# The last projection of a mixer walks its weight blocks outermost and its token tiles innermost

## The chip, the cores and the metric

The kernel runs on 1 core of a Trainium2 chip. The metric is the device time of one execution in microseconds; the median of 3 runs is given. A smaller time is better.

## What is computed

One layer of a decoder for 256 tokens with 1024 channels: a mixer (a gated convolution branch and a differential attention branch, whose gated sum goes through a last projection `w_o`), and then a feed-forward part with 32 experts, of which each token takes 4. What matters for this case is the seam between the two:

```
mix = (sigmoid(g_conv) * y_conv + sigmoid(g_attn) * y_attn) @ W_o
x   = x + gate1 * mix
h2  = RMSNorm(x) * (1 + scale2) + shift2
x   = x + gate2 * MoE(h2)     # top-4 of 32 experts, clamped SwiGLU,
                              # softmax over the selected router logits
```

Everything is in 32-bit floats.

## The kernel before

The 256 tokens are two tiles of 128 (`TT = 2`, index `tt`). Weights pass through one large area of SBUF, cut into 11 slots of 2 MB each. In the mixer, weight blocks of 1024 x 512 go round in six of these slots; `w_o` is the last two blocks, `WO0` and `WO0 + 1`, each with one half of the 1024 output columns. After the mixer the slots take the experts' weights: an expert has six chunks of 2 MB, four of `w_up` and two of `w_down`, so 192 chunks come in through the queue of SyncE, in a fixed order, each when its slot is free.

The order of the work is written by hand. Each engine has its own program, and semaphores join them. The list `order` numbers the uses of four PSUM banks; use n takes bank n % 4, `bank_full` tells that TensorE has filled it and `bank_free` that it was read. The four `w_o` results are uses `WO_USE` to `WO_USE + 3`.

What happens around the last projection, engine by engine:

- TensorE transposes the mixed tokens (line 1241), then makes the four results of `w_o` (line 1253, 8 matmuls of 128x512 each, which the trace records as 16): tile 0 with block 0, tile 0 with block 1, tile 1 with block 0, tile 1 with block 1. Then for each token tile: it copies x into the output accumulators by two matmuls with the identity (line 1261), waits for h2 of this tile, transposes h2 (line 1269, 8 transposes), waits for ScalarE's copies, and makes the router logits (line 1276, recorded as 16 matmuls of 32 columns). After both tiles come the routing steps (lines 1283 to 1313), and then the loop over units of at most 32 tokens of an expert (lines 1321 to 1386).
- VectorE multiplies each `w_o` result by the gate (line 939) and adds it to x (line 941). In the same pass over the tiles it finishes the norm: reciprocal (944), scale (945), shift (947). So the h2 steps of tile 0 stand ahead of the `w_o` results of tile 1. After both tiles it makes the second gate (951) and the routing from the logits (956 on).
- ScalarE squares and sums x of a tile (655), takes the square root (657), copies the transposed h2 of this tile (661), and goes to the next tile only then.
- SyncE's queue issues the experts' chunks. After chunks 0 to 5 it waits until block `WO0` was used and loads chunk 6, waits until `WO0 + 1` was used and loads chunk 7, waits for the second gate (`gate2_ready`) and loads chunk 8, waits for the last transpose of h2 and loads chunk 9, and waits for the routing's result (`units_ready`) and loads chunk 10. From chunk 11 on, each load waits until TensorE has used the chunk that lay in its slot, in the loop over the units.

The result of the gate multiply lies in `conv_acc`, of which the version before uses two parts in turn.

Of the kernel before, what the change touches and what calls it, by code (L numbers as in the profile page):

```python
# [24 lines left out]
ALU = mybir.AluOpType  # L25
# [5 lines left out]
TT = T // P  # L31
# [39 lines left out]
def build(nc, x, c, positions, w_ada, b_ada, norm1_g, w_in, conv_w, conv_b, conv_ln_g, conv_ln_b,  # L71
# [3 lines left out]
    with ctx:  # L75
# [3 lines left out]
        def sem(name):  # L79
            return ctx.enter_context(nc.semaphore(name))  # L80
# [5 lines left out]
        def slot(i, a=0, b=BLOCKF):  # L86
            return W[:, BLOCKF * i + a:BLOCKF * i + b]
# [11 lines left out]
        conv_acc = slot(X_SLOT, 0, 2 * D).rearrange("p (k t) -> p k t", k=KD)  # L99
        x_tok = slot(X_SLOT, 2 * D).rearrange("p (t d) -> p t d", t=TT)  # L100
# [3 lines left out]
        def small(shape, dt=F32):  # L104
# [131 lines left out]
            sem(n) for n in ("on_ready", "lam_arg"))  # L236
        conv_done, csq_ready, ln_ready, sw_sig, swish_ready = (
            sem(n) for n in ("conv_done", "csq_ready", "ln_ready", "sw_sig", "swish_ready"))
        gate_ready, mixed, x1_ready, h2_ready = (
            sem(n) for n in ("gate_ready", "mixed", "x1_ready", "h2_ready"))  # L240
        lg_ready, tw_ready, routed_ready, comb_ready, m_ready, oh_ready, units_ready = (
            sem(n) for n in ("lg_ready", "tw_ready", "routed_ready", "comb_ready", "m_ready",
                             "oh_ready", "units_ready"))
# [34 lines left out]
        WO0 = len(blocks)  # L278
# [3 lines left out]
        def place(n):  # L282
            return (n + SHIFT) % RING

        def blk(n, k=KD):
            return W[:, place(n) * BLOCKF:(place(n) + 1) * BLOCKF].rearrange("p (k n) -> p k n", k=k)
# [4 lines left out]
        def used_by(n, use):  # L291
            used[n] = (bank_full[use % 4], use // 4 + 1)
# [44 lines left out]
        WO_USE = use_of["w_o", 0]  # L337
# [9 lines left out]
        def gate_use(h):  # L347
            return use_of["gate", h]
# [16 lines left out]
        for i in range(2):  # L365
            used_by(ADA0[i] + 3, ADA_USE[i])
            used_by(V0 + i, V_USE + 2 * i + 1)
            used_by(COUT0 + i, YC_USE[2 * i + 1])
            used_by(AOUT0 + i, YA_USE + 2 * i + 1)
            used_by(WO0 + i, WO_USE + 2 + i)  # L370

        def bank(use):
            return PS[use % 4]

        def full(eng, use):
            eng.wait_ge(bank_full[use % 4], use // 4 + 1)

        def fill(pe, use):
            if use >= 4:
                pe.wait_ge(bank_free[use % 4], use // 4)  # L380
# [139 lines left out]
        def _(act_e):  # L520
# [86 lines left out]
            for h in range(HEADS):  # L607
                par = h % 2
                act_e.wait_ge(s_max, h + 1)
                for part in range(2):  # L610
                    sc = PS[4 + 2 * par + part]
                    for blk_q, (a, b) in enumerate(((0, P), (P, 3 * P))):
                        at = 2 * blk_q + part
# [4 lines left out]
                use = gate_use(h)  # L618
# [32 lines left out]
            load(norm2_b, norm2_g.to_broadcast([P, D]), in_norm2)  # L651

            for tt in range(TT):
                act_e.wait_ge(x1_ready, 2 * tt + 2)
                s.activation(buf_c[:, tt, :], x_tok[:, tt, :], ACT.Square, accum_out=ssq[:, tt:tt + 1]).then_inc(x_ssq, 1)
                act_e.wait_ge(x_ssq, TT + 2 + 2 * tt)
                s.activation(rstd[:, tt:tt + 1], ssq[:, tt:tt + 1], ACT.Sqrt, scale=1.0 / D, bias=eps[:]).then_inc(x_ssq, 1)
                for i in (2 * tt, 2 * tt + 1):
                    use = H2T_USE[i]
                    full(act_e, use)  # L660
                    s.copy(h2T[:, 4 * (i % 2):4 * (i % 2) + 4, P * tt:P * tt + P],
                           bank(use)[:, :].rearrange("p (k t) -> p k t", k=4)).then_inc(bank_free[use % 4], 1)
# [28 lines left out]
        def _(dve):  # L691
            v = nc.vector
            n = 0

            def step(ins):
                nonlocal n
                n += 1
                ins.then_inc(dve_step, 1)
                dve.wait_ge(dve_step, n)
# [43 lines left out]
            for k, (turn, add) in enumerate(((0.25, TWO_PI / 4), (0.0, 0.0))):  # L743
                r, t = rope[:, 4 + k, :, :], rope[:, 1, :, :]
# [76 lines left out]
            for i in range(8):  # L821
                use = QK_USE + i
                tt, col, which = i % 2, NB * ((i // 2) % 2), i // 4
# [39 lines left out]
            for h in range(HEADS):  # L863
                par = h % 2
                dve.wait_ge(sc_full, h + 1)
                for blk_q, (a, b) in enumerate(((0, P), (P, 3 * P))):
                    for part in range(2):
                        at = 2 * blk_q + part
# [52 lines left out]
            for i in range(4):  # L921
                use = YA_USE + i
# [7 lines left out]
            dve.wait_ge(mod_ready, 16 * 16)  # L930
            dve.wait_ge(in_norm2, 16)
            step(v.scalar_tensor_tensor(modb[:, 2, :], modb[:, 2, :], 1.0, norm2_b, ALU.add, ALU.mult))
            for tt in range(TT):
                for half in range(2):
                    cs = slice(NB * half, NB * half + NB)
                    use = WO_USE + 2 * tt + half
                    full(dve, use)
                    gated = conv_acc[:, 2 * half:2 * half + 2, :].rearrange("p a t -> p (a t)")
                    v.tensor_tensor(gated, bank(use)[:, :], modb[:, 0, cs], ALU.mult).then_inc(bank_free[use % 4], 1)
                    dve.wait_ge(bank_free[use % 4], use // 4 + 1)  # L940
                    v.tensor_tensor(x_tok[:, tt, cs], x_tok[:, tt, cs], gated, ALU.add).then_inc(x1_ready, 1)

                dve.wait_ge(x_ssq, TT + 3 + 2 * tt)
                step(v.reciprocal(rstd[:, tt:tt + 1], rstd[:, tt:tt + 1]))
                step(v.scalar_tensor_tensor(h2[:, tt, :], x_tok[:, tt, :], rstd[:, tt:tt + 1], modb[:, 2, :],
                                            ALU.mult, ALU.mult))
                v.tensor_tensor(h2[:, tt, :], h2[:, tt, :], modb[:, 1, :], ALU.add).then_inc(h2_ready, 1)
# [5 lines left out]
            for tt in range(TT):  # L953
                use = LG_USE[tt]
# [108 lines left out]
        def _(pe):  # L1063
            t = nc.tensor

            def wait_block(n):
                pe.wait_ge(blk_full[place(n)], 16 * loads_before[n])
# [33 lines left out]
            for k in range(KD):  # L1101
                use, n0 = CONV_USE + k, CONV0 + 2 * (k // 4)
# [35 lines left out]
            for i in range(8):  # L1138
                use = QKT_USE + i
# [34 lines left out]
            for h in range(HEADS):  # L1174
# [13 lines left out]
                n = GATE0 + h // 2  # L1188
# [32 lines left out]
            for i in range(4):  # L1221
                use = OT_USE + i
# [12 lines left out]
            for i in range(4):  # L1235
                use = MT_USE + i
# [3 lines left out]
                    kk = 4 * (i % 2) + k  # L1240
                    ins = t.transpose(bank(use)[:, P * k:P * k + P], gates[:, i // 2, P * kk:P * kk + P], ident[:])
                ins.then_inc(bank_full[use % 4], 1)
            wait_block(WO0)
            wait_block(WO0 + 1)
            for i in range(4):
                use = WO_USE + i
                fill(pe, use)
                tt, n = i // 2, WO0 + i % 2
                if n == WO0:
                    for j in (2 * tt, 2 * tt + 1):  # L1250
                        pe.wait_ge(bank_free[(MT_USE + j) % 4], (MT_USE + j) // 4 + 1)
                for k in range(KD):
                    ins = t.matmul(bank(use)[:, :], mixT[:, k, P * tt:P * tt + P], blk(n)[:, k, :],  # L1253
                                   start=(k == 0), stop=(k == KD - 1))
                ins.then_inc(bank_full[use % 4], 1)
            pe.wait_ge(in_moe, 16)
            for tt in range(TT):

                pe.wait_ge(x1_ready, 2 * tt + 2)
                for i in range(2):  # L1260
                    t.matmul(Y[tt][i][:, :], ident[:], x_tok[:, tt, NB * i:NB * i + NB], start=True, stop=True,
                             skip_group_check=True)
                pe.wait_ge(h2_ready, tt + 1)
                for i in (2 * tt, 2 * tt + 1):
                    use = H2T_USE[i]
                    fill(pe, use)
                    for k in range(4):
                        kk = 4 * (i % 2) + k
                        ins = t.transpose(bank(use)[:, P * k:P * k + P], h2[:, tt, P * kk:P * kk + P], ident[:])
                    ins.then_inc(bank_full[use % 4], 1)  # L1270
                for i in (2 * tt, 2 * tt + 1):
                    pe.wait_ge(bank_free[H2T_USE[i] % 4], H2T_USE[i] // 4 + 1)
                use = LG_USE[tt]
                fill(pe, use)
                for k in range(KD):
                    ins = t.matmul(bank(use)[:, 0:EXPERTS], h2T[:, k, P * tt:P * tt + P], wr[:, k, :],
                                   start=(k == 0), stop=(k == KD - 1))
                ins.then_inc(bank_full[use % 4], 1)
# [142 lines left out]
```

## Time and profile before

| what | value |
|---|---|
| median of 3 runs | 1333.82 us (1333.71 to 1333.87) |
| the profiled execution's own time | 1331.9 us |
| its span | 1330.0 us |
| mean granted clock of TensorE | 0.937 |
| TensorE matmul busy | 1130.1 us, 85% |
| TensorE weight loads busy | 434.6 us, 33% |
| VectorE busy | 376.1 us, 28% |
| ScalarE busy | 231.5 us, 17% |
| HBM read | 473.83 MB |

A span is the time from the first to the last recorded instruction; the execution's own time has some 2 us around it. Busy shares are means over stages that differ: the mixer takes roughly the first 400 us, the experts the rest. A granted clock of 1.00 is TensorE's upper level (2.4 GHz), 0.50 its lower (1.2 GHz).

### The profile page before, as it was taken

Reading aid. Unit: us, or ns where it says so; the run is one execution under the profiler, and the core shown is the slowest. Engines: PE = TensorE matmul, PEld = TensorE weight load, DVE = VectorE, ACT = ScalarE, POOL = GpSimd, SP = SyncE. Lnnn points to the kernel's source line nnn. Section 1 sums busy time; section 2 is a strip of 40 time slices with the busy share of each in tenths; the row PEclk is TensorE's granted clock in tenths of the full one; section 3 lists DMA queues with packets and bytes.
Section 4 is the critical chain, followed back from the end, with each engine's and each line's share of the span. In section 5 each row is a group of like instructions: output and inputs, shape, how many; then the busy total and the mean of one; then the engine's idle time right before and its main releaser. Section 6 shows DMA issues by size and latency. Waiting matters only on the chain.

```text
span 1330.0 us, 18351 instructions
## 1 busy us (share of the span) xinstructions
PE 1130.1 (85%) x7535; PEld 434.6 (33%) x7535; DVE 376.1 (28%) x1042; ACT 231.5 (17%) x448; POOL 48.7 (4%) x76
## 2 busy tenths in 40 slices
PE   2899999999989767757999766997869796999996
PEld 0584445444443212112333211332213131333331
DVE  0399956651252111010221111211101120212221
ACT  1200013460022101100122011111101111111220
POOL 2100000036100000000000000000000000000000
PEclk7899999999988988788999988998889898999998
DMA  9938694166569999999999999999999999599997
GB/s 316 363 146 308 261 340 166 64 191 224 209 253 367 423 425 426 426 426 427 426 426 423 425 426 427 424 424 426 426 424 424 425 427 426 239 406 421 422 427 315
DMA packets 65217, 477.81 MB, mean 359 GB/s; under 512 B 6680, under 2 KB 6713, under 8 KB 29322
## 3 DMA queue, kind: packets, MB, share of 16 engines
q1 hardware_dynamic: 61028, 472.14, 86.8%
q0 software_dynamic: 1200, 3.28, 1.0%
q10 hardware_dynamic: 2934, 1.58, 0.5%
q8 instruction: 45, 0.74, 0.2%
q14 instruction: 10, 0.08, 0.0%
HBM read 473.83 MB, written 1.05 MB: 357 GB/s over the span
## 4 chain that ended last, share of the span: by engine, by line
PE 53%; DMA 25%; SPq 16%; ACT 3%; DVE 2%; issue 1%; DVEq 0%
DMA weights<-in_w_down 19%; SPq L404 15%; PE bank L1359 15%; PE bank L1118 10%; PE bank L1386 8%; PE bank L1108 4%; PE bank L1334 4%; DMA weights<-in_w_in 3%; DMA weights<-in_w_up 3%; PE bank L1194 3%; PE bank L1253 2%; PE bank L1321 2%; PE bank L1341 1%; PE bank L1327 1%; ACT buf_d L681 1%
## 5 line engine op out<-in xcount | busy, mean ns | idle before, releaser
L1359 PE MATMUL bank<-weights,buf_d 128*32 128x512 f32 x3008 | 390.9, 666 | 134.1 <-DMA weights<-in_w_up 134.1
L1359 PEld LDWEIGHTS bank<-weights,buf_d 128*32 128x32 f32 x3008 | 97.0, 117 | 404.0 <-DMA weights<-in_w_up 202.2
L1386 PE MATMUL bank<-weights,buf_d 128*32 128x512 f32 x1504 | 174.7, 598 | 10.3 <-DMA weights<-in_w_down 10.1
L1047 DVE TENSOR_SCALAR u_conv<-bank 128x256 f32<-128x256 f32 x47 | 20.0, 425 | 460.2 <-PE bank L1359 460.2
L679 ACT ACTIVATE u_conv<-u_conv 128x256 f32<-128x256 f32 x47 | 19.6, 416 | 642.4 <-DVE u_conv L1047 642.4
L1334 PE MATMUL bank<-buf_d 64*128 64x512 f32 x384 | 99.8, 639 | 0.9 <-DVE buf_d L1057 0.9
L797 DVE SCALAR_TENSOR_TENSOR weights<-u_conv,weights 128x256 f32<-128x256 f32 x240 | 96.9, 480 | 0.3
L1057 DVE TENSOR_TENSOR buf_d<-bank,u_conv 128x512 f32<-128x512 f32 x47 | 32.5, 692 | 225.4 <-PE bank L1386 225.4
L1118 PE MATMUL bank<-weights,buf_d 128*128 128x512 f32 x192 | 82.9, 593 | 1.0 <-DMA weights<-in_w_in 1.0
L1386 PEld LDWEIGHTS bank<-weights,buf_d 128*32 128x32 f32 x1504 | 42.4, 109 | 107.2 <-issue 81.4
L1321 PE MATMUL bank<-buf_c,u_conv 128*32 128x256 f32 x768 | 60.4, 387 | 1.1 <-DVE u_conv L1016 1.1
L1108 PE MATMUL bank<-buf_d,weights 128*128 128x256 f32 x256 | 57.3, 388 | 3.9 <-DMA weights<-in_w_in 3.9
L679 ACT ACT_TABLE_LOAD x47 | 60.3, 1283 | 0.8
L1334 PEld LDWEIGHTS bank<-buf_d 64*128 64x128 f32 x384 | 35.1, 198 | 75.2 <-issue 75.2
L1194 PE MATMUL bank<-weights,buf_d 128*128 128x512 f32 x128 | 57.4, 592 | 0.0
L1108 PEld LDWEIGHTS bank<-buf_d,weights 128*128 128x128 f32 x256 | 49.7, 195 | 11.3 <-issue 4.1
L1118 PEld LDWEIGHTS bank<-weights,buf_d 128*128 128x128 f32 x192 | 36.3, 190 | 47.7 <-issue 45.8
L1327 PE MATMUL bank<-ident,buf_d 128*128 128x128 f32 x190 | 48.0, 335 | 4.0 <-ACT buf_d L674 0.5
L1074 PE MATMUL bank<-weights 128*32 128x512 f32 x192 | 26.6, 703 | 27.3 <-DMA weights<-in_w_ada 27.3
L1327 PEld LDWEIGHTS bank<-ident,buf_d 128*128 128x128 f32 x190 | 29.8, 206 | 33.2 <-issue 19.4
L1341 PE MATMUL bank<-late,u_conv 96*32 96x512 bf16 x282 | 37.8, 391 | 0.5 <-ACT buf_d L676 0.5
L681 ACT COPY buf_d<-bank 128x256 f32<-128x256 f32 x47 | 17.5, 373 | 110.1 <-PE bank L1321 110.1
(260 smaller groups left out, 757.0 us busy)
## 6 DMA issues: line engine op xcount, KB each, us to landing
weights<-in_w_up SPq DMA_DIRECT2D x128, 2048.0 KB, 33.7
weights<-in_w_down SPq DMA_DIRECT2D x64, 2048.0 KB, 37.2
weights<-in_w_in SPq DMA_DIRECT2D x14, 2048.0 KB, 18.4
weights<-in_w_ada SPq DMA_DIRECT2D x12, 2048.0 KB, 18.8
weights<-in_w_conv_out SPq DMA_DIRECT2D x2, 2048.0 KB, 11.6
weights<-in_w_attn_out SPq DMA_DIRECT2D x2, 2048.0 KB, 7.7
weights<-in_w_o SPq DMA_DIRECT2D x2, 2048.0 KB, 10.8
weights<-late POOLq DMA_DIRECT2D x16, 128.0 KB, 3.8
```

The costliest lines, as they stand in the source:

```text
L404: sp.dma_start(dst, src).then_inc(w_full[chunk_slot(e, j)], 16)
L679: s.activation(sg, glu, ACT.Sigmoid, scale=ALPHA).then_inc(sg_ready, 1)
L797: ins = v.scalar_tensor_tensor(acc, u_conv[:, k, w:w + T], convw[:, k, w:w + 1], acc, ALU.mult, ALU.add)
L1108: ins = t.matmul(bank(use)[:, T * half:T * half + T], blk(n0 + half)[:, kk, P * (k % 4):P * (k % 4) + P], h1T[:, kk, :], start=(kk == 0), ...
L1118: ins = t.matmul(bank(use)[:, :], lhsT[:, k, P * tt:P * tt + P], blk(n)[:, k, :], start=(k == 0 and bias is None), stop=(k == KD - 1))
L1194: ins = t.matmul(bank(gate_use(h))[:, :], h1T[:, k, P * par:P * par + P], blk(n)[:, k, :], start=False, stop=(k == KD - 1))
L1321: ins = t.matmul(GX[SLOTS * g:SLOTS * g + SLOTS, 0:T], pick[:, tt, :], h2[:, tt, T * g:T * g + T], start=(tt == 0), stop=(tt == TT - 1))
L1327: ins = t.transpose(bank_[:, at + P * r:at + P * r + P], src.rearrange("p (c r) -> p r c", r=2)[:, r, :], ident[:])
L1334: ins = t.matmul(Y[tt][i][:, :], Cmb[rows, P * tt:P * tt + P], oe[rows, :], start=False, stop=True, skip_group_check=True)
L1341: t.matmul(bank_[SLOTS * g:SLOTS * g + SLOTS, :], sel, ebias[:, col + NB * n_:col + NB * n_ + NB], start=True, stop=False)
L1359: ins = t.matmul(UP[SLOTS * g:SLOTS * g + SLOTS, :], xgT[:, r, SLOTS * j:SLOTS * j + SLOTS], w[:, r, NB * g:NB * g + NB], start=False, sto ...
L1386: ins = t.matmul(DOWN[rows, :], actT[:, r, at:at + SLOTS], w[:, g, r, NB * i:NB * i + NB], start=(r == 1 and h == 0 and g == 0), stop=(h = ...
```

## The change

TensorE makes the four `w_o` results in the order tile 0 with block 0, tile 1 with block 0, tile 0 with block 1, tile 1 with block 1, and waits for the second block only ahead of the third result. VectorE follows the same order in its multiplies and adds, and its h2 steps move into a loop of their own behind all four. Since the tiles' x are now completed in turns, the semaphore `x1_ready` becomes two, one for each tile. Block `WO0` counts as used after the second result (before: the third), `WO0 + 1` after the fourth as before. The gate's products get four places in `conv_acc` in place of two. The number of instructions and of bytes does not change, but for the semaphores.

```diff
@@ who has used a block last
-            used_by(WO0 + i, WO_USE + 2 + i)
+            used_by(WO0 + i, WO_USE + 2 * i + 1)
@@ ScalarE
             for tt in range(TT):
-                act_e.wait_ge(x1_ready, 2 * tt + 2)
+                act_e.wait_ge(x1_ready[tt], 2)
@@ VectorE
-            for tt in range(TT):
-                for half in range(2):
+            for half in range(2):
+                for tt in range(TT):
                     cs = slice(NB * half, NB * half + NB)
-                    use = WO_USE + 2 * tt + half
+                    use = WO_USE + 2 * half + tt
                     full(dve, use)
-                    gated = conv_acc[:, 2 * half:2 * half + 2, :].rearrange("p a t -> p (a t)")
+                    at = 4 * half + 2 * tt
+                    gated = conv_acc[:, at:at + 2, :].rearrange("p a t -> p (a t)")
                     v.tensor_tensor(gated, bank(use)[:, :], modb[:, 0, cs], ALU.mult).then_inc(bank_free[use % 4], 1)
                     dve.wait_ge(bank_free[use % 4], use // 4 + 1)
-                    v.tensor_tensor(x_tok[:, tt, cs], x_tok[:, tt, cs], gated, ALU.add).then_inc(x1_ready, 1)
-
+                    v.tensor_tensor(x_tok[:, tt, cs], x_tok[:, tt, cs], gated, ALU.add).then_inc(x1_ready[tt], 1)
+            for tt in range(TT):
                 dve.wait_ge(x_ssq, TT + 3 + 2 * tt)
                 step(v.reciprocal(rstd[:, tt:tt + 1], rstd[:, tt:tt + 1]))
@@ TensorE
-            wait_block(WO0)
-            wait_block(WO0 + 1)
             for i in range(4):
                 use = WO_USE + i
                 fill(pe, use)
-                tt, n = i // 2, WO0 + i % 2
+                tt, n = i % 2, WO0 + i // 2
+                if tt == 0:
+                    wait_block(n)
                 if n == WO0:
@@
-                pe.wait_ge(x1_ready, 2 * tt + 2)
+                pe.wait_ge(x1_ready[tt], 2)
```

## Rows read from the trace of the kernel before

**Rows 1.** The chain that ended last: start us, us, what.

```profile
349.26 27.47 PE bank L1253 x64
...
386.06 1.96 PE bank L1276 x16
399.39 1.97 PE bank L1321 x16
```

**Rows 2.** Windows: stretch, length, busy time of each engine, granted clock, DMA share, GB/s.

```profile
396.00:398.80 2.80, 2.29 (x10) 2.10 (x10) 1.11 (x4) 0.00 (x0) 0.00 (x0) 0.50 0.18 76
...
406.00:408.00 2.00, 2.00 (x20) 0.54 (x16) 0.00 (x0) 0.00 (x0) 0.00 (x0) 0.80 0.00 0
...
440.00:780.00 340.00, 268.22 (x2084) 81.76 (x2076) 52.51 (x160) 48.51 (x80) 0.00 (x0) 0.91 1.01 426
780.00:1130.00 350.00, 282.28 (x2216) 87.20 (x2220) 54.31 (x165) 51.54 (x85) 0.00 (x0) 0.91 1.01 425
1130.00:1160.00 30.00, 29.85 (x268) 10.39 (x264) 6.56 (x20) 6.06 (x10) 0.00 (x0) 1.00 0.64 272
```

**Rows 3.** Timeline of SyncE's queue: start us, us, issue, count.

```profile
369.89 0.34 SPq L404 DMA_DIRECT2D weights<-in_w_up  x1
...
376.75 9.00 SPq L404 DMA_DIRECT2D weights<-in_w_up  x3
398.85 0.38 SPq L404 DMA_DIRECT2D weights<-in_w_down  x1
...
407.05 0.38 SPq L404 DMA_DIRECT2D weights<-in_w_down  x1
```

**Rows 4.** Timeline of VectorE, 364 to 384 us.

```profile
364.60 0.69 DVE L941 TENSOR_TENSOR weights<-weights 128x512 f32<-128x512 f32 x1
...
377.49 0.69 DVE L941 TENSOR_TENSOR weights<-weights 128x512 f32<-128x512 f32 x1
381.40 0.16 DVE L944 RECIPROCAL weights<-weights 128x1 f32<-128x1 f32 x1 [3.21 <-ACT weights L657]
...
382.92 1.22 DVE L947 TENSOR_TENSOR buf_c<-buf_c,weights 128x1024 f32<-128x1024 f32 x1
```

**Rows 5.** Timeline of ScalarE, 378 to 381 us.

```profile
378.92 1.07 ACT L661 COPY buf_d<-bank 128x512 f32<-128x512 f32 x2 [10.84 <-PE bank L1269]
379.88 1.07 ACT L655 ACTIVATE buf_c<-weights 128x1024 f32<-128x1024 f32 x1
```

**Rows 6.** Timeline of TensorE's matmuls, 376 to 398 us.

```profile
376.56 1.88 PE L1261 MATMUL bank<-weights,ident 128*128 128x512 f32 x4
378.28 1.04 PE L1269 MATMUL bank<-ident,buf_c 128*128 128x128 f32 x8
380.09 1.94 PE L1276 MATMUL bank<-weights,buf_d 128*128 128x32 f32 x16 [0.77 <-ACT buf_d L661]
381.87 1.96 PE L1261 MATMUL bank<-weights,ident 128*128 128x512 f32 x4
384.19 1.09 PE L1269 MATMUL bank<-ident,buf_c 128*128 128x128 f32 x8 [0.37 <-DVE buf_c L947]
386.06 1.94 PE L1276 MATMUL bank<-weights,buf_d 128*128 128x32 f32 x16 [0.77 <-ACT buf_d L661]
390.25 0.37 PE L1283 MATMUL bank<-weights 128*32 128x1 f32 x4 [2.25 <-DVE weights L966]
...
397.35 0.95 PE L1313 MATMUL bank<-u_conv,buf_d 32*128 32x64 f32 x4
```

**Rows 7.** Timeline of TensorE's matmuls around an idle gap in the loop.

```profile
747.57 1.90 PE L1359 MATMUL bank<-weights,buf_d 128*32 128x512 f32 x16
752.24 3.25 PE L1359 MATMUL bank<-weights,buf_d 128*32 128x512 f32 x16 [2.77 <-DMA weights<-in_w_up]
```

**Rows 8.** Windows of TensorE alone: matmul busy, granted clock, DMA share, GB/s.

```profile
388.00:389.50 1.50, 0.00 (x1) 1.00 1.04 448
390.00:393.00 3.00, 2.13 (x8) 0.50 1.00 426
```

More of the change, by code:

```diff
@@ L238, in build @@
             sem(n) for n in ("conv_done", "csq_ready", "ln_ready", "sw_sig", "swish_ready"))
-        gate_ready, mixed, x1_ready, h2_ready = (
-            sem(n) for n in ("gate_ready", "mixed", "x1_ready", "h2_ready"))
+        gate_ready, mixed, h2_ready = (sem(n) for n in ("gate_ready", "mixed", "h2_ready"))
+        x1_ready = [sem(f"x1_tile{tt}_ready") for tt in range(TT)]
         lg_ready, tw_ready, routed_ready, comb_ready, m_ready, oh_ready, units_ready = (
```

## The prediction

> **What bounds the kernel now.** I read the chain that ended last first, to see whether the place of the change lies on it. It does: the chain runs through the 64 matmuls of the last projection, then the logits of tile 1, then the first unit of the expert loop [rows 1]. Then I read windows over the DMA engines, since the experts' weights are most of the traffic. From 440 to 1130 us the engines are full (share 1.01, 425 to 426 GB/s), while TensorE is busy some 80% [rows 2]: there the weight stream sets the pace. From 1130 to 1160 the roles change: TensorE is busy 29.85 of 30 us and the DMA share drops to 0.64 [rows 2]. Neither part can make up for a late start. The stream of the loop begins when TensorE frees its first chunks, and the stretch in which TensorE leads begins with weights that the stream brought late by the same amount. So the question is when the stream starts, and two windows answer it: at 396 to 398.8 us the DMA share is 0.18, and at 406 to 408 it is 0.00 [rows 2]. All that was loaded ahead has landed, the engines are idle, and the steady stream starts with the issue at 407.05, which waits for TensorE's use of the first chunk in unit 0 [rows 3]. Whatever delays unit 0 delays the end by the same time; what lands before it buys nothing.
>
> **What the change adds and moves.** No work is added or removed. Three things move.
>
> *The early load.* Block `WO0` is free after the second result and no longer after the third. The 64 matmuls take 27.5 us [rows 1], so one result takes 6.9 us, and the load of chunk 6 moves from 369.89 [rows 3] to about 363.0. The next load, at 376.75, waits for the other block, which is used last as before. The DMA engines stand idle later anyway (share 0.18 at 396 [rows 2]), so the gain is 0. I cost it at nothing, and the cover is that idle time.
>
> *Tile 0's norm.* Before, x of tile 0 was complete at 364.60 + 0.69 = 365.3 [rows 4], and its whole norm was made behind the matmuls of tile 1. After, x of tile 0 is complete with the third result: that ends at 349.1 + 3 x 6.9 = 369.8, and multiply and add take it to 371.3. Square and root on ScalarE still fit before the fourth result ends at 376.7. But VectorE's h2 steps of tile 0 now stand behind the fourth multiply and add, which end at 377.49 + 0.69 = 378.2 [rows 4]. From the start of the reciprocal to the end of the shift takes 382.92 + 1.22 - 381.40 = 2.74 us [rows 4]. So h2 of tile 0 is ready at 378.2 + 2.8 = 381.0. TensorE would have taken it at 378.28 [rows 6], behind its two copies of x. It now idles for 2.7 us.
>
> *Tile 1's norm goes along.* ScalarE's square of tile 1 stands behind its copies of tile 0's transposes: they start at 378.92, the square at 379.88 [rows 5]. The transposes start 2.74 us later, so the copies, the square, the root, VectorE's three steps and the transposes of tile 1 (384.19 before [rows 6]) all come 2.74 us later, at 386.9. From the logits of tile 1 on, everything is in series (logits 386.06, first routing matmul 390.25 [rows 6]). With the clock as before the sum is +2.7 us.
>
> *The clock.* With this the sum is not done. The granted clock was 1.00 at 388 to 389.5 us and 0.50 at 390 to 393 [rows 8]: it fell in the wait of 2.25 us behind the narrow logits matmuls [rows 6], at about 389.7. A row in the loop shows how short a gap is enough: behind 2.77 us without a matmul, 16 matmuls took 3.25 us where the 16 before the gap took 1.90 [rows 7]. The new gap is 2.7 us, and what follows it is thin: 8 transposes of 1.04 us, a wait of 0.77 us, and 16 logits matmuls of 32 columns [rows 6]. Before, no gap there was over 0.77 us [rows 6]. So I expect that the clock falls to 1.2 GHz soon behind the gap, about when the logits of tile 0 start, at 380.09 + 2.74 = 382.8. The trace has no such logits at the lower level; the nearest row is four matmuls with 128-column weight loads in 0.95 us [rows 6], 0.235 each, so 16 take 3.7 us where they took 1.94. The bounds for them are 1.94 (nothing lost) and 2 x 1.94 = 3.9. Then come the two copies of x for tile 1: four matmuls spaced 0.43 us (27.47 us for 64 [rows 1]), so about 1.8 us of streaming, and 3.4 at half the clock. The row from the loop has a ratio of 1.7 and holds a part at the upper level [rows 7], so its 3.1 us is the lower bound and 3.5 the upper.
>
> The path is then: logits of tile 0 from 382.8 to 386.5, copies of x to 389.9. The transposes of tile 1 would be ready to go at 386.9, so TensorE itself is now the last: they start at 389.9 in place of 384.19, 5.7 us late. The copies of x are a dense stream, and I expect the clock to come back behind them, so the transposes (1.09) and logits (1.94) of tile 1 keep their price, apart from a tail of the logits at the lower level, which I put at 0.3 us of the 0 to 1.8 that all of them could lose. The routing ran at the lower clock before [rows 8] and costs the same. The sum is 5.7 + 0.3 = +6.0 us.
>
> The Trainium skill, "TensorE: Matmul & The Clock Gate", section "HAM oscillation — how this bites in real kernels", gives a practical limit to idle gaps, and a gap of 2.7 us is within it: by that rule nothing falls and the time is that of the first rival below. Rows 7 speak against it, since there the clock was lower behind a gap no longer than this one.
>
> **The forecast.** The profiled execution took 1331.9 us for a span of 1330.0, and the shift is the same in both: the sum gives 1337.9 for such an execution. The median of the runs stands 1.9 us above it at 1333.8, so I forecast 1333.8 + 6.0 = 1339.8 us.
>
> **The rivals.**
>
> A. The clock holds, for the new gap is just short enough or the transposes behind it are enough work. Then only VectorE's order counts: +2.7 us, 1336.5. For it: a gap of 2.7 us is no longer than gaps in the loop, some of which the clock may survive. Against it: rows 7, and the thin work behind the gap. It lies on the bound of 0.2% (2.7 us).
>
> B. The clock falls at once and does not come back before the routing. Then the transposes of tile 0 take 2.1, their logits 3.7, the copies of x 3.4, the transposes of tile 1 2.1 and their logits 3.7, with two waits of 0.77: 381.0 + 16.5 = 397.5 for the end of the logits, which was 388.0: +9.5 us, 1343.3. For it: the thin work in all of this stretch. Against it: 3.4 us without any gap in its middle.
>
> C. It gets faster. The earlier load of chunk 6 would do it: if the loads ahead of the loop were a backlog that the loop had to wait for, 2 MB more out of the way would save up to 2.1 MB / 425 GB/s = 4.9 us, and against the 2.7 of rival A the net is -2.2 us, 1331.6. The point from which it decides: the DMA engines would have to be busy without a break from 385 to the first unit. They are idle at 396 to 398.8 and 406 to 408 [rows 2], and a shift of 3 us of their issues only widens that.
>
> D. The shift is hidden: the DMA stream of the loop might not be bound to its start, if TensorE's 20% of idle time held a reserve. 1333.8. Against it: with a share of 1.01 for 690 us [rows 2] the bytes have nowhere to go.
>
> **How the numbers follow.** My chances: the forecast (+4 to +8) 0.62; A 0.17; B and what lies between it and the forecast 0.10; C 0.05; D 0.06. What a measurement can tell from no change is about 0.2%, 2.7 us. A falls on that bound, so I give 0.07 of it to "same" and 0.10 to "slower". Faster is C: 0.05. Same is D and that part of A: 0.13. Slower is the rest: 0.82. The range reaches down to A, 1336.4, and up to +8.0 us, 1341.8, short of B's full price; it leaves out C, D, the top of B and some of A.
>
> **What would show it.** In the profile after: the fourth add of line 941 still near 377.5, and the reciprocal of tile 0 at 378.2 right behind it; a gap of 2.7 us before the transposes of tile 0 at 381.0; granted clock 0.50 in the windows around 383 to 389, and the 16 logits matmuls of tile 0 at 3.4 to 3.9 us; the transposes of tile 1 near 390, waiting for no VectorE step; the issue that starts the stream at 413 in place of 407.05; a chunk issued at 363.0; and DMA shares of 1.0 as before from there on. If the transposes of tile 1 start at 386.9, rival A is right. If the clock falls elsewhere than I think, by a microsecond or two, the price moves between 4 and 8 us. The forecast would be wrong altogether if the executions that are timed have the clock's fall at another place than the profiled one, before or after.

## The result and the profile after

The changed kernel took 1340.26 us (median of 6 executions, 1337.34 to 1340.63), the kernel before 1333.76 (6 executions beside it, 1333.22 to 1334.28). The ratio is 1.0046, with a 95% interval from 1.0033 to 1.0058: slower by 6.5 us. On two later occasions, beside its own runs of the kernel before each time, it took 1337.35 against 1333.07 and 1338.57 against 1332.84, a ratio of 1.0042 in both (1.0029 to 1.0056, and 1.0029 to 1.0054). The interval stays above 1 each time, though the change is only some 0.45%.

The profiled execution took 1340.44 us for a span of 1338.5. It is read from TensorE's timeline first (start us, us, line, what), which answers to [rows 6].

```profile
377.71 1.88 PE L1262 MATMUL bank<-weights,ident 128*128 128x512 f32 x4
382.04 1.97 PE L1270 MATMUL bank<-ident,buf_c 128*128 128x128 f32 x8 [2.45 <-DVE buf_c L948]
384.73 3.59 PE L1277 MATMUL bank<-weights,buf_d 128*128 128x32 f32 x16 [0.72 <-issue]
388.13 3.76 PE L1262 MATMUL bank<-weights,ident 128*128 128x512 f32 x4
391.68 1.19 PE L1270 MATMUL bank<-ident,buf_c 128*128 128x128 f32 x8
393.65 1.99 PE L1277 MATMUL bank<-weights,buf_d 128*128 128x32 f32 x16 [0.77 <-ACT buf_d L661]
397.88 0.37 PE L1284 MATMUL bank<-weights 128*32 128x1 f32 x4 [2.25 <-DVE weights L967]
```

The whole picture is moved by 1.15 us, since the copies of x for tile 0 start at 377.71 and not at 376.56: this execution had come to `w_o` that much later. Counted from this start, the transposes of tile 0 begin 4.33 us on (before 1.72), those of tile 1 13.97 us on (before 7.63), and the first routing matmul 20.17 us on (before 13.69): 6.5 us later. There are two parts. A new wait of 2.45 us stands ahead of the transposes of tile 0, for VectorE's shift (line 948). Behind it, everything up to the copies of x for tile 1 takes about twice its former time: 1.97 against 1.04, 3.59 against 1.94, 3.76 against 1.96.

The timelines of VectorE and of ScalarE around the wait (these answer to [rows 4, 5]):

```profile
378.64 0.69 DVE L942 TENSOR_TENSOR weights<-weights 128x512 f32<-128x512 f32 x1
379.25 0.16 DVE L945 RECIPROCAL weights<-weights 128x1 f32<-128x1 f32 x1
...
380.76 1.22 DVE L948 TENSOR_TENSOR buf_c<-buf_c,weights 128x1024 f32<-128x1024 f32 x1
386.03 0.16 DVE L945 RECIPROCAL weights<-weights 128x1 f32<-128x1 f32 x1 [4.05 <-ACT weights L657]
...
387.55 1.22 DVE L948 TENSOR_TENSOR buf_c<-buf_c,weights 128x1024 f32<-128x1024 f32 x1
```

```profile
374.95 0.29 ACT L657 ACTIVATE weights<-weights 128x1 f32<-128x1 f32 x1
383.19 0.59 ACT L661 COPY buf_d<-bank 128x512 f32<-128x512 f32 x1 [7.94 <-PE bank L1270]
384.04 0.58 ACT L661 COPY buf_d<-bank 128x512 f32<-128x512 f32 x1 [0.27 <-PE bank L1270]
384.52 1.06 ACT L655 ACTIVATE buf_c<-weights 128x1024 f32<-128x1024 f32 x1
```

The root of tile 0 was done at 375.2, and its reciprocal starts only at 379.25, right behind the fourth add: VectorE's own order held it for 4 us. h2 of tile 1 was ready at 387.55 + 1.22 = 388.8, and TensorE took it at 391.68. By then TensorE itself was late.

Windows of TensorE alone (matmul busy, granted clock, DMA share, GB/s), which answer to [rows 8]:

```profile
381.00:382.00 1.00, 0.00 (x0) 0.88 1.03 442
383.00:384.00 1.00, 1.00 (x5) 0.50 0.92 393
388.00:390.00 2.00, 2.00 (x5) 0.50 0.00 0
392.00:393.00 1.00, 0.88 (x8) 1.00 0.94 377
396.00:398.00 2.00, 0.12 (x2) 0.50 1.02 434
```

The clock went to its lower level inside the wait, at about 381.8, stayed there through the copies of x, was back at 392 and fell once more before the routing. SyncE's queue, and the weight stream behind it (windows with the busy time of TensorE, its weight loads, VectorE, ScalarE and GpSimd), answer to [rows 2, 3]:

```profile
364.17 29.06 SPq L404 DMA_DIRECT2D weights<-in_w_up  x4
...
414.71 0.38 SPq L404 DMA_DIRECT2D weights<-in_w_down  x1
```

```profile
402.00:406.00 4.00, 3.22 (x14) 2.49 (x12) 1.94 (x9) 0.63 (x2) 0.00 (x0) 0.50 0.00 0
...
446.00:780.00 334.00, 264.42 (x2080) 81.67 (x2076) 51.01 (x155) 48.46 (x80) 0.00 (x0) 0.91 1.01 426
```

The first chunk behind `w_o` is now issued at 364.17, early as the change says. It buys nothing: the DMA engines stand idle at 402 to 406. The issue that starts the steady stream comes at 414.71 in place of 407.05, 7.66 us later. Of this, 1.15 us is this execution's later start of the copies of x, and 6.5 us came behind it. From there the stream runs as before, at share 1.01 and 426 GB/s.

### The profile page after: what moved, and what is told of

The parts are those of the page before. It is cut to its first block, busy times and chain, and to the rows that moved or that the text cites. A ratio compares the mean times of both kernels' runs of the same rounds, so it can differ in the third digit from the quotient of the medians.

```text
span 1338.5 us, 18352 instructions
## 1 busy us (share of the span) xinstructions
PE 1138.1 (85%) x7535; PEld 441.5 (33%) x7535; DVE 374.6 (28%) x1042; ACT 231.3 (17%) x448; POOL 48.5 (4%) x76
## 4 chain that ended last, share of the span: by engine, by line
PE 54%; DMA 23%; SPq 16%; ACT 3%; DVE 2%; issue 1%; DVEq 0%; ACTq 0%
SPq L404 16%; DMA weights<-in_w_down 15%; PE bank L1360 15%; PE bank L1119 10%; PE bank L1387 8%; DMA weights<-in_w_up 5%; PE bank L1109 4%; PE bank L1335 4%; DMA weights<-in_w_ada 2%; PE bank L1254 2%; PE bank L1195 2%; PE bank L1322 2%; PE bank L1342 1%; PE bank L1328 1%; PE bank L1075 1%
```

## The experiments

Each was timed in five rounds beside the kernel before. Extra matmuls in them are real work whose results are overwritten; no run leaves out a part of the computation. There were three occasions, each on another chip. The first had the gap filled, h2 between the adds, VectorE's part alone and the late release (before: 1333.08). The second had the changed kernel and the late release once more, the copies behind the logits with the routing filled, and only the routing filled (before: 1333.07). The third had the changed kernel a third time, the copies moved alone, and more waits filled (before: 1332.84).

**The gap filled.** The changed kernel with six more matmuls in the new wait:

```diff
+                if tt == 0:
+                    fill(pe, H2T_USE[0])
+                    for _ in range(6):
+                        t.matmul(bank(H2T_USE[0])[:, 0:256], ident[:], x_tok[:, 0, 0:256], start=True, stop=True,
+                                 skip_group_check=True)
                 pe.wait_ge(h2_ready, tt + 1)
...
-                    fill(pe, use)
+                    if i:
+                        fill(pe, use)
```

> The changed kernel with six more matmuls of 128x256 (their results are overwritten) on TensorE between its two copies of x for tile 0 and its wait for h2 of tile 0, some 2.6 us of work in a gap of 2.7. My theory: the clock holds, logits of tile 0 take 1.94 us again, the transposes of tile 1 start 2.7 us later than before instead of 6, and the kernel takes 1336.3 to 1337.0 (3 to 4 us under the changed kernel). Rival, that the order of VectorE and the in-order queue of ScalarE carry all the loss and the clock is a side show: no gain over the changed kernel, 1340. Second rival, that the extra matmuls push the transposes back: 1340 or more.

It took 1335.21 us, ratio 1.0015 (1.0006 to 1.0024), +2.1 us. TensorE's timeline and the clock in it:

```profile
378.24 2.75 PE L1267 MATMUL bank<-weights,ident 128*128 128x256 f32 x12
380.85 1.09 PE L1276 MATMUL bank<-ident,buf_c 128*128 128x128 f32 x8
382.72 1.94 PE L1283 MATMUL bank<-weights,buf_d 128*128 128x32 f32 x16 [0.77 <-ACT buf_d L661]
384.50 1.96 PE L1262 MATMUL bank<-weights,ident 128*128 128x512 f32 x4
386.82 1.09 PE L1276 MATMUL bank<-ident,buf_c 128*128 128x128 f32 x8 [0.36 <-DVE buf_c L948]
```

```profile
380.00:390.00 10.00, 8.09 (x53) 1.00 0.50 177
```

The transposes of tile 0 start as late as without the filler (4.32 us behind the start of the copies of x, before 4.33), but the clock stays at 1.00 over the whole window and every group has its old duration to within 0.05 us. The transposes of tile 1 start at 386.82, which is 2.63 us behind [rows 6], and they wait for VectorE again. More work on TensorE made the kernel faster: its interval (up to 1.0024) lies below those of the changed kernel (from 1.0029). What is left, 2 to 2.7 us, is the order on VectorE; the rest of the loss was the clock. The measured 1335.21 is a median of 11 and lies 1.1 us under the span that I gave. The kernel before took 1333.08 here and not 1333.8, which is 0.7 of it; the rest is that the order cost 2.1 us and not 2.7.

**h2 of tile 0 back between the adds.** The changed kernel, with `w_o`'s blocks outermost, and VectorE's three steps taken into the loop:

```diff
                     v.tensor_tensor(x_tok[:, tt, cs], x_tok[:, tt, cs], gated, ALU.add).then_inc(x1_ready[tt], 1)
-            for tt in range(TT):
-                dve.wait_ge(x_ssq, TT + 3 + 2 * tt)
+                    if half == 0:
+                        continue
+                    dve.wait_ge(x_ssq, TT + 3 + 2 * tt)
... (the three steps follow, moved into the loop)
```

> The changed kernel with VectorE's three h2 steps of tile 0 between the adds of the third and the fourth w_o result, so only the blocks of w_o stay outermost. My theory: h2 of tile 0 is ready at about 377, ahead of the end of the copies of x, so there is no gap, the clock holds, and the time is that of the kernel before within 0.5 us: 1333.3 to 1334.3. Rival, that the order of the w_o results itself (x of tile 0 complete one result later) costs part of the loss: 1335 to 1337.

It took 1332.99 us, ratio 0.9999 (0.9990 to 1.0008): no difference from before. The absolute span that I gave was 0.3 us too high, since the kernel before took 1333.08 here. VectorE's timeline, then TensorE's:

```profile
376.64 1.23 DVE L949 TENSOR_TENSOR buf_c<-buf_c,weights 128x1024 f32<-128x1024 f32 x1
377.78 0.68 DVE L940 TENSOR_TENSOR weights<-bank,weights 128x512 f32<-128x512 f32 x1
```

```profile
377.54 1.88 PE L1263 MATMUL bank<-weights,ident 128*128 128x512 f32 x4
379.26 1.04 PE L1271 MATMUL bank<-ident,buf_c 128*128 128x128 f32 x8
```

h2 of tile 0 is ready at 377.9, ahead of the end of the copies of x, and no wait is left. The new order of the matmuls costs nothing by itself that this run can tell.

**VectorE's part alone.** The kernel before, tiles outermost on TensorE, with one line added on VectorE:

```diff
                     v.tensor_tensor(x_tok[:, tt, cs], x_tok[:, tt, cs], gated, ALU.add).then_inc(x1_ready, 1)
 
+            for tt in range(TT):
                 dve.wait_ge(x_ssq, TT + 3 + 2 * tt)
```

> The kernel before (token tiles outermost on TensorE) with VectorE's h2 steps of both tiles moved behind all four adds. My theory: the loss comes from this move alone, so the time is that of the changed kernel, 1339 to 1341. Rival, that the new order of the w_o results is needed for the loss: 1334 to 1336.

It took 1339.58 us, ratio 1.0050 (1.0036 to 1.0064). This one line has the whole loss. TensorE's timeline shows the same picture as after the change:

```profile
381.75 1.97 PE L1270 MATMUL bank<-ident,buf_c 128*128 128x128 f32 x8 [2.44 <-DVE buf_c L948]
384.44 3.59 PE L1277 MATMUL bank<-weights,buf_d 128*128 128x32 f32 x16 [0.72 <-issue]
```

**The early load undone, and the changed kernel again.**

```diff
-            used_by(WO0 + i, WO_USE + 2 * i + 1)
+            used_by(WO0 + i, WO_USE + 2 + i)
```

> The changed kernel with block WO0 counted as used after the third w_o result and no longer the second: chunk 6 is loaded 6.9 us later, as before. My theory: the early load gains nothing, so 1340 within 0.7 us, as the changed kernel. Rival, that the early load saved up to 4.9 us and hid a part of the loss: 1342 to 1345.

It took 1337.28 us, ratio 1.0037 (1.0023 to 1.0051), 3 us less than the changed kernel had taken on its own occasion. I had expected the same time, so I ran both once more, side by side.

> The changed kernel once more, on the same chip as the next run. Expected 1340 within 1 us if its time is a property of the kernel; single executions near 1337, as one was before, would show a fall of the clock at a later moment (383 to 384.5 us).

> The changed kernel with the later release of block WO0, once more. It took 1337.3, 3 us less than the changed kernel, and in its profile the clock fell at 384.4 and not at 381.9. My theory: the release costs and gains nothing and only the moment of the clock's fall differed by chance, so this run and e5_after_again agree within 1 us. Rival: the early release costs 3 us (a load that starts at 363 in place of 370), and the two differ by 3 us again.

The changed kernel took 1337.35 us, 2.65 below the 1340 that I had expected, and the one with the late release 1336.86: the difference of 3 us did not come back. So the early load neither gains nor costs anything that these runs can tell. What had differed was the clock. TensorE's timelines, first of the changed kernel in this run, then of the late release in its first:

```profile
380.76 1.09 PE L1270 MATMUL bank<-ident,buf_c 128*128 128x128 f32 x8 [2.45 <-DVE buf_c L948]
382.62 2.67 PE L1277 MATMUL bank<-weights,buf_d 128*128 128x32 f32 x16 [0.77 <-ACT buf_d L661]
...
388.66 1.91 PE L1270 MATMUL bank<-ident,buf_c 128*128 128x128 f32 x8
```

```profile
381.32 1.09 PE L1270 MATMUL bank<-ident,buf_c 128*128 128x128 f32 x8 [2.45 <-DVE buf_c L948]
383.19 2.63 PE L1277 MATMUL bank<-weights,buf_d 128*128 128x32 f32 x16 [0.77 <-ACT buf_d L661]
```

The wait of 2.45 us is the same, but the transposes of tile 0 kept the upper level (1.09 in place of 1.97), and the logits lost only 0.7 us in place of 1.65. On the other hand the transposes of tile 1 now took 1.91 us in place of 1.19. These two executions took 1336.52 and 1337.28. A third run of the changed kernel asked whether the moment belongs to the occasion or the chip:

> The changed kernel a third time. Its median was 1340.3 in six executions and 1337.4 in five on another occasion. If the moment of the clock's fall is drawn anew for each execution, both values come up again among these; if it belongs to the chip or the occasion, all five lie near one of the two.

Its five executions took 1339.79, 1338.19, 1338.57, 1337.71 and 1340.0, median 1338.57. They are spread over the span between the two values, so single executions differ on one occasion as well; the first occasion, with five of six between 1339.86 and 1340.63, also differs from the second, with four of five between 1336.52 and 1337.65. No chip was used on two of the three occasions of the experiments, so these runs can't tell a chip from an occasion.

**The same lever in the other direction.** If a later start costs one to one, an earlier one must gain. The kernel before with its copies of x behind the logits of each tile. Chunk 9 goes into the slot in which x lies, so its load now waits for the first routing result:

```diff
@@ TensorE, in the loop over the tiles
-                pe.wait_ge(x1_ready, 2 * tt + 2)
-                for i in range(2):
-                    t.matmul(Y[tt][i][:, :], ident[:], x_tok[:, tt, NB * i:NB * i + NB], start=True, stop=True,
-                             skip_group_check=True)
                 pe.wait_ge(h2_ready, tt + 1)
...
                 ins.then_inc(bank_full[use % 4], 1)
+                for i in range(2):
+                    t.matmul(Y[tt][i][:, :], ident[:], x_tok[:, tt, NB * i:NB * i + NB], start=True, stop=True,
+                             skip_group_check=True)
@@ SyncE
-            full(sp, H2T_USE[3])
+            full(sp, TOT_USE)
             load_chunk(1, 3)
```

> The kernel before with TensorE's copies of x for each tile moved behind this tile's logits, without any filler. With fillers as well it took 1328.5. My theory: the move alone takes h2 of tile 1 some 1.5 us earlier and leaves the lower clock in the routing, so 1330.5 to 1332. Rival, that the move carries nearly all of the gain: 1328 to 1329.5; that it carries none, since the clock falls earlier with it: 1333 or more.

It took 1330.24 us, ratio 0.9980 (0.9971 to 0.9988), just under the span that I gave. TensorE's timeline, and a window in the routing:

```profile
388.03 3.66 PE L1276 MATMUL bank<-weights,ident 128*128 128x512 f32 x4
391.62 0.29 PE L1282 MATMUL bank<-weights 128*32 128x1 f32 x4
...
396.54 0.55 PE L1312 MATMUL bank<-u_conv,buf_d 32*128 32x64 f32 x4
```

```profile
396.00:397.00 1.00, 1.00 (x10) 1.00 1.11 475
```

The copies of tile 1 now lie in the former wait of 2.25 us. They took 3.66 us, since the clock fell again at 388.1, so the first routing matmul did not come earlier: it stands 14.26 us behind TensorE's first matmul after `w_o` (377.36 here), where it stood 13.69 behind it before [rows 6]. But the clock was back at 391.5, and the routing ran at the upper level. From its first matmul to the end of its last it took 391.62 to 397.09, 5.5 us, where it had taken 390.25 to 398.30, 8.05 us [rows 6]. That is where the gain lies, and my theory, which left the routing at the lower clock, was wrong on it.

With overwritten matmuls in the waits of the routing besides:

```diff
+            def warm(use, n):
+                for _ in range(n):
+                    t.matmul(PS[use % 4][:, 0:256], ident[:], h2[:, 0, 0:256], start=True, stop=True,
+                             skip_group_check=True)
...
+            fill(pe, END_USE)
+            warm(END_USE, 3)
             pe.wait_ge(m_ready, 1)
-            fill(pe, END_USE)
...
+            fill(pe, UN_USE)
+            warm(UN_USE, 1)
             pe.wait_ge(bank_free[RT_USE % 4], RT_USE // 4 + 1)
             pe.wait_ge(oh_ready, 1)
-            fill(pe, UN_USE)
...
+            warm(UN_USE + 1, 2)
             pe.wait_ge(units_ready, 2)
```

> The kernel before, with TensorE's copies of x for a tile moved behind the logits of this tile (chunk 9 of the weights then waits for the first routing matmul), and six overwritten matmuls of 128x256 in the waits of the routing. My theory, that the end follows the start of the loop one to one: h2 of tile 1 is taken 1.5 us earlier, the gap of 2.25 us behind the logits is filled by the copies, and the clock stays at 1.00 into the first unit, which saves 1.9 us on its first chunk and 2 to 3 us on the routing: 1327 to 1330. Rival, that the DMA stream has a reserve or the early units do not bind: 1333.

It took 1328.54 us, ratio 0.9965 (0.9951 to 0.9978). This interval overlaps that of the copies moved alone, so these two runs do not show what the fillers of the routing add. TensorE's timeline, and windows:

```profile
379.58 1.94 PE L1277 MATMUL bank<-weights,buf_d 128*128 128x32 f32 x16 [0.77 <-ACT buf_d L661]
381.36 3.30 PE L1281 MATMUL bank<-weights,ident 128*128 128x512 f32 x4
...
402.21 7.05 PE L1366 MATMUL bank<-weights,buf_d 128*32 128x512 f32 x64
```

```profile
382.00:385.00 3.00, 3.00 (x7) 0.50 0.86 366
392.20:404.00 11.80, 9.92 (x80) 1.00 0.85 306
```

Unit 0 now runs at the upper level from its first chunk. But the clock had fallen at 381.8 for a while, behind a wait of 0.77 us. So one more of these matmuls went into each such wait, ahead of the logits:

```diff
+                use = LG_USE[tt]
+                fill(pe, use)
+                warm(use, 1)
                 for i in (2 * tt, 2 * tt + 1):
                     pe.wait_ge(bank_free[H2T_USE[i] % 4], H2T_USE[i] // 4 + 1)
-                use = LG_USE[tt]
-                fill(pe, use)
```

> The kernel with the copies moved and the routing filled, with one more overwritten matmul of 128x256 in each wait of 0.77 us ahead of the logits. There the clock had fallen at 381.9 us though no gap was longer than 0.8 us. My theory: with these waits filled the clock holds through both tiles, the copies of x take 1.96 us each, and the start of the stream comes 1.5 to 3 us earlier than without: 1325.5 to 1327.5. Rival, that the filler does not keep it up: 1328 to 1329.5.

It took 1326.34 us, ratio 0.9954 (0.9941 to 0.9967), the lowest median here. Beside the copies moved alone, on the same occasion (1330.24), all fillers together gave 3.9 us; against the version one step before, the intervals overlap. The times fall into two groups, four from 1325.58 to 1326.6 and two at 1330.32 and 1330.72. The profiled one is of the second group: the copies of x for tile 0 are back at 1.96 us, but the clock fell near 395, before unit 0.

```profile
380.75 1.96 PE L1282 MATMUL bank<-weights,ident 128*128 128x512 f32 x4
```

```profile
395.20:404.00 8.80, 7.81 (x40) 0.50 0.77 287
```

That the clock holds into unit 0 in the first group would fit, but no execution of that group was profiled.

**Only the routing filled.** The kernel before with its copies of x in their old place, five of the overwritten matmuls ahead of the first routing wait, and the six in the later waits of the routing as above:

```diff
+            fill(pe, TOT_USE)
+            warm(TOT_USE, 5)
             pe.wait_ge(routed_ready, 1)
-            fill(pe, TOT_USE)
... (the six as above)
```

> The kernel before with eleven overwritten matmuls of 128x256 in TensorE's waits between the logits and the first unit, and nothing else. My theory: the clock stays at 1.00 there, the routing and the first chunk take 3 to 5 us less, 1328.5 to 1330.5. Rival, that the clock of this stretch does not matter for the end: 1333 to 1334; that the fillers get in the way of the routing matmuls: 1334 to 1336.

It took 1331.57 us, ratio 0.9992 (0.9983 to 1.0001): short of what I expected, and unclear against before. The first five fillers came too late and then stood in the way. TensorE's timeline:

```profile
388.88 3.92 PE L1258 MATMUL bank<-buf_c,ident 128*128 128x256 f32 x10
392.74 0.29 PE L1289 MATMUL bank<-weights 128*32 128x1 f32 x4
```

The clock had fallen at 388.6, at the end of the logits, just ahead of them. So the five matmuls (10 records) took 3.9 us, where they would take 2.3 at the upper level by the 12 records in 2.75 us of the filled gap. The logits ended at 389.1, and the routing would have begun 2.25 us later [rows 6], at 391.3; it began at 392.74, pushed back by 1.4 us.

**Start of the stream against the end.** The issue of chunk 11, which starts the steady stream, and the own time of each profiled execution:

| kernel | issue, us | own time, us | difference |
|---|---|---|---|
| copies moved, routing filled | 404.18 | 1329.67 | 925.49 |
| copies moved | 405.57 | 1330.69 | 925.12 |
| more filled | 405.73 | 1330.32 | 924.59 |
| routing filled | 406.44 | 1331.06 | 924.62 |
| before | 407.05 | 1331.9 | 924.85 |
| h2 between the adds | 408.49 | 1333.22 | 924.73 |
| gap filled | 408.92 | 1333.75 | 924.83 |
| changed, second run | 411.75 | 1336.52 | 924.77 |
| late release, second run | 412.03 | 1336.76 | 924.73 |
| late release | 412.31 | 1337.28 | 924.97 |
| changed, third run | 414.04 | 1339.79 | 925.75 |
| VectorE's part alone | 414.42 | 1339.48 | 925.06 |
| changed | 414.71 | 1340.44 | 925.73 |

The issue moves by 10.5 us over the thirteen kernels and runs, and the difference stays between 924.6 and 925.8.

## Why the prediction was right

**What bounds the kernel.** I read from the idle DMA engines ahead of the loop that any delay of unit 0 would reach the end in full. The table shows it, in both directions, and rival D, a reserve in the stream, has it against it.

**The early load** was costed at 0 behind the idle DMA engines. The chunk was issued early, and its release put back made no difference side by side (1336.86 against 1337.35). Rival C, which needed a backlog of loads, has the windows at 402 to 406 against it.

**Tile 0's norm.** I gave 2.74 us for VectorE's steps behind the fourth add. The transposes of tile 0 came 2.6 us later, and with the clock held up the kernel lost 2.1 us. VectorE's line alone had the whole loss, and the line put back had none.

**The clock.** I expected it to fall where the logits of tile 0 start. In the first profile it fell some 2 us earlier (381.8, where my 382.8 is 384.0 with this execution's 1.15), inside the wait, so the transposes of tile 0 paid too, 0.9 us that the sum did not have. The logits took 3.59 (I had 3.7) and the copies of x 3.76 (I had 3.4, and an upper bound of 3.5, though twice my own 1.8 is 3.6). In this profile the clock was back behind the copies of x, as I had it. The tail of tile 1's logits, for which I had put 0.3 us, cost 0.05. Counted from start to start, the loss is 2.6 us for the wait, 0.9 for the transposes of tile 0, 1.6 for its logits, 1.2 for the copies and 0.15 for tile 1: 6.5 to the first routing matmul. The sum had 2.7, 0, 1.9, 1.1 and 0.3, 6.0. What it lacked in one term it had too much of in others, so that it came this near is in part luck. In the second run the clock fell at 383.6, and the same count gives 2.6, 0.05, 0.7, 1.2 and, since the clock was not yet back for the transposes of tile 1, 0.8: 5.4. The start of the stream came 4.8 us later by that count, since the clock was back sooner within unit 0, and the median was 4.3 us above before. All three medians lie in the range; the size of this term hangs on a moment that I had fixed with no row to fix it. The loop's row, too, had been chosen from one side. Other rows of the kernel before:

```profile
455.63 1.92 PE L1359 MATMUL bank<-weights,buf_d 128*32 128x512 f32 x16 [2.96 <-DMA weights<-in_w_up]
...
480.23 1.92 PE L1359 MATMUL bank<-weights,buf_d 128*32 128x512 f32 x16 [2.75 <-DMA weights<-in_w_up]
```

From 440 to 1130 us, 30 groups of 16 records of this line stand behind a wait for the DMA of 2.7 to 3.0 us; 23 took 2.73 to 3.59 us, and seven kept 1.92. So that row showed that such a gap can cost the clock, not that it must.

**The rivals.** A, with the clock up, is what the run with the filled gap took: +2.1 where I had +2.7. It was not the kernel as changed in any of the profiled executions. B, the lower clock through both tiles, did not come up: in each profile of the gap unfilled the clock was back at about the end of the copies of x or during the transposes behind them. C, a gain, is answered above.

**The page's rule.** The Trainium skill, "TensorE: Matmul & The Clock Gate", section "HAM oscillation — how this bites in real kernels", would have let the gap of 2.45 us pass; here the clock fell inside it or within 3.1 us of its end in all six profiled executions that had it unfilled, so the measurement decides. In the seven loop rows with 1.92 the gap did pass. The section "A second HAM failure mode: psum-queue depth-cycling" of the same page tells of short pauses between groups of matmuls that bring the clock down and up again. The trace of the kernel with the copies moved and the routing filled agrees: with no wait over 0.77 us the clock was at 0.50 from 382 to 385 and at 1.00 again from 385.3 to 388.6. The kernel before had the same waits and kept 1.00 until 389.7.

## What to carry to other kernels

When a loop is reordered on one engine, look at what the other engines' in-order programs put behind it: here the matmuls could be reordered for nothing, and three small VectorE steps that slid behind the last add cost everything. A weight stream that is full to its end turns each microsecond ahead of its first issue into one of the whole, so the serial stretch before it is the place to work on, and loads that land before it are not. Price a new wait on TensorE at the lower clock for what stands behind it as well, and put real work that is due anyway into such waits, then look at where it pays: the copies of x in their new place gave 2.6 us (1330.24 against 1332.84), through a routing at the upper level and not through an earlier one.

## What was not expected of the hardware

- The clock fell with no wait longer than 0.8 us. In the kernel with the copies moved and the routing filled, the copies of x right behind the logits of 32 columns took 3.30 us where they had taken 1.96. Ahead of the fall at 381.8 TensorE had made eight transposes, waited 0.77 us and made these logits. What of this brought the clock down was not taken apart.
- The same kernel paid between 4 and 6.5 us for the same wait, by when the clock fell behind it: at 381.8 and 383.6 in two profiled executions of the changed kernel. Executions of the kernel before lay within some 3 us (1331.44 to 1334.64 over the three occasions of the experiments), those of the changed kernel within 4.3 (1336.52 to 1340.8). Why one occasion gave mostly the one and another mostly the other is open: only one execution of each run was profiled, and each of the three occasions of the experiments had another chip.
- The changed kernel's profiled executions at 1340 have a difference of 925.7 in the table against 924.8 for most others. What takes this last microsecond behind the start of the stream was not looked for.
